# First expert tile's rows gathered from the route stage, with three weight matrices loaded behind that gather

## The reference, cut to what matters

```python
g_w, g_idx = lax.top_k(softmax(h @ w_gr + b_gr), 1)          # 1 of 4 groups
top_v, top_i = lax.top_k(softmax(e_logits of that group), 2) # 2 of its 8 experts
for e in range(32):
    hid = silu(h @ w_gate[e]) * (h @ w_up[e])                # 1024 -> 256
    out = out + combine[:, e:e+1] * (hid @ w_down[e])        # 256 -> 1024
```

## Time and profile before

| what | us |
|---|---|
| median of three runs | 1039.96 (1038.82 to 1040.89) |
| the profiled execution's own time | 1040.27 |
| its span, first to last recorded instruction | 1038.5 |
| route stage of layer 0, to the barrier | about 216.4 to 239.7 |
| expert stage of layer 0, until its pair rows are read back | about 239.7 to 488.9 |
| route stage of layer 1, to the barrier | about 740.7 to 763.6 |
| expert stage of layer 1, with the outputs | about 763.6 to 1038.5 |

### The profile page before, as it was taken

The page is one execution under the profiler, slowest core; times in us unless marked ns, Lnnn a source line. Parts: engine busy times, 40 slices in busy tenths (PEclk is TensorE's granted clock), DMA queues, the critical chain, the costliest instruction groups (busy, mean ns, idle before and its releaser), DMA issues. The chain is left out here.

```text
span 1038.5 us, 18756 instructions
## 1 busy us (share of the span) xinstructions
PE 906.1 (87%) x7250; PEld 658.1 (63%) x7250; DVE 414.2 (40%) x955; ACT 287.7 (28%) x595; POOL 293.3 (28%) x438
## 2 busy tenths in 40 slices
PE   7999999974999889875799999989849998887885
PEld 6988888963555555542687878579745555545553
DVE  5366784255111111111768878773552111111114
ACT  6356673131111111110532112362302111111103
POOL 1810000013343343211052527720123443443110
PEclk9999999996999999999589999999969999999997
DMA  7612111777999999996824636315869999999966
GB/s 234 187 36 52 51 42 54 272 300 295 373 416 416 417 413 415 418 420 237 266 67 127 159 85 159 92 50 220 359 256 362 414 415 418 416 415 419 420 277 254
DMA packets 112277, 277.71 MB, mean 267 GB/s; under 512 B 34952, under 2 KB 73176, under 8 KB 88074
## 3 DMA queue, kind: packets, MB, share of 16 engines
q1 hardware_dynamic: 96630, 253.74, 64.2%
q0 software_dynamic: 11424, 17.87, 4.7%
q10 hardware_dynamic: 4132, 4.86, 1.9%
HBM read 266.25 MB, written 27.45 MB: 283 GB/s over the span
## 5 line engine op out<-in xcount | busy, mean ns | idle before, releaser
L2106 DVE COPY areaB<-ps 128x512 f32<-128x512 f32 x66 | 45.6, 691 | 344.7 <-PE ps L2089 344.7
L2072 PE MATMUL ps<-ring,areaB 128*64 128x256 f32 x576 | 139.4, 397 | 24.6 <-issue 20.5
L2073 PE MATMUL ps<-ring,areaB 128*64 128x256 f32 x576 | 139.8, 398 | 0.0
L2118 POOL DMA_INDIRECT pair_rows<-areaB,idx x66 | 67.7, 1026 | 246.5 <-DVE areaB L2106 238.4
L2072 PEld LDWEIGHTS ps<-ring,areaB 128*64 128x64 f32 x576 | 79.0, 142 | 64.8 <-issue 25.2
L2097 ACT ACTIVATE v_rows<-ps 128x256 f32<-128x256 f32 x66 | 25.3, 384 | 256.5 <-PE ps L2073 256.5
L1058 PE MATMUL ps<-conv_x_high,pw_halves 128*128 128x272 f32 x512 | 90.1, 297 | 1.8 <-DVE areaS L1293 1.8
L2113 POOL DMA_INDIRECT areaC<-h_rows,idx x66 | 68.8, 1042 | 64.2 <-issue 45.8
L2094 ACT ACTIVATE areaB<-ps 128x512 f32<-128x512 f32 x66 | 39.4, 597 | 156.4 <-PE ps L2062 156.4
L2073 PEld LDWEIGHTS ps<-ring,areaB 128*64 128x64 f32 x576 | 79.0, 143 | 0.0
L2089 PE MATMUL ps<-ring,areaB 128*64 128x512 f32 x320 | 76.1, 593 | 2.7 <-DVE areaB L2103 1.6
(11 more groups left out here) (379 smaller groups left out, 1893.9 us busy)
## 6 DMA issues: line engine op xcount, KB each, us to landing
ring<-in_w_down SPq DMA_DIRECT2D x40, 1024.0 KB, 23.9
ring<-in_w_gate SPq DMA_DIRECT2D x32, 1024.0 KB, 23.7
ring<-in_w_up SPq DMA_DIRECT2D x32, 1024.0 KB, 26.4
wring<-in_w_down SPq DMA_DIRECT2D x12, 1024.0 KB, 25.7
areaS<-in_w_down SPq DMA_DIRECT2D x12, 1024.0 KB
wring<-in_w_pw SPq DMA_DIRECT2D x24, 512.0 KB, 4.6
areaA<-in_w_gate SPq DMA_DIRECT2D x10, 1024.0 KB, 27.1
areaA<-in_w_up SPq DMA_DIRECT2D x10, 1024.0 KB, 29.3
```

What stands on the lines that cost most here:

```text
L2072: pe.matmul(ps[0:CAP, 2 + odd, 0:F], rows, ring_gate(ws)[:, k, :], start=(k == 0), stop=(k == KT - 1))
L2073: mm = pe.matmul(ps[CAP:P, 2 + odd, 0:F], rows, ring_up(ws)[:, k, :], start=(k == 0), stop=(k == KT - 1))
L2106: return v.tensor_copy(rows_out[:, s, :], ps[:, 5 + odd, :])
L2118: return gp.indirect_dma_start(pair_half_rows, bass.IndirectOffsetOnAxis(idx[:, RING + s:RING + 1 + s], 0), rows_out[:, s, :], None, bound ...
```

## The change

GpSimd now issues tile 0's gather in the route stage, behind waits for the five stores and for `first_numbers`. That semaphore is raised by a new VectorE instruction which casts the first four columns of `tok_of` into `idx`, and stands between L1658 and L1659. In the expert stage GpSimd no longer casts for tiles 0 to 3, whose gathers follow each other without waits. SP no longer asks for down 4 and for gate and up 5 in the route stage; it does so first thing in the expert stage, after tile 0's gather has landed.

```diff
-        def half_row_numbers(v, steps, number, n, at):
+        def half_row_numbers(v, steps, number, n, at, first_numbers=None):
...
             steps.link(v.tensor_scalar(toks, toks, 2.0, half_col, ALU.mult, ALU.add))
+            if first_numbers:
+                v.tensor_copy(idx[:, 0:RIN], toks[:, 0:RIN]).then_inc(first_numbers, 1)
             steps.link(v.tensor_scalar(pairs, pairs, 2.0, half_col, ALU.mult, ALU.add))
...
+        def gather_rows(gp, s):
+            return gp.indirect_dma_start(rows_in[:, s, :], None, h_half_rows, bass.IndirectOffsetOnAxis(idx[:, s:s + 1], 0),
+                                         bounds_check=2 * T - 1, oob_is_err=False)
...
                     load_gateup(sp, l, 4, 4)
-                    load_down(sp, l, 4, 4)
-                    sp.wait_ge(h_stored, 16 * NT)
-                    load_gateup(sp, l, RING, RING)
...
                     gp.wait_ge(filled, 5)
+                    gp.wait_ge(h_stored, 16 * NT)
+                    gp.wait_ge(first_numbers, 1)
+                    gather_rows(gp, 0).then_inc(first_gathered[l], 16)
...
+                    sp.wait_ge(gathered[0], 16)
+                    load_down(sp, l, 4, 4)
+                    load_gateup(sp, l, RING, RING)
                     sp.wait_ge(fullest_ready, 1)
...
                     def fetch(x):
-                        after(gp, gathered[x.at], 16 * x.turns)
-                        fill_idx(gp, x.at, x.e, tok_ready, tok_of if x.e < RING else tok_seq, 0)
-                        after(gp, turned, x.e - RIN + 1)
-                        gp.wait_ge(tok_ready, x.e + 1)
-                        gather(gp, x.at).then_inc(gathered[x.at], 16)
+                        if x.turns:
+                            gp.wait_ge(gathered[x.at], 16 * x.turns)
+                            fill_idx(gp, x.at, x.e, tok_ready, tok_of if x.e < RING else tok_seq, 0)
+                            gp.wait_ge(turned, x.e - RIN + 1)
+                            gp.wait_ge(tok_ready, x.e + 1 - RIN)
+                            settle(gp, pool_settled)
+                        gather_rows(gp, x.at).then_inc(gathered[x.at], 16)
...
-                    for e in range(AHEAD):
+                    for e in range(1, AHEAD):
```

More of the change, by code:

```diff
@@ L1662, in hybrid_step, with make_table @@
         table = lambda bank: ps[:, bank, 256:256 + NE]
-        def make_table(v, steps, match_ready, table_made, n):
+        def make_table(v, steps, match_ready, table_made, n, first_numbers=None):
             match_slots(v, rank, match_ready)
             v.wait_ge(table_made, n + 1)
-            half_row_numbers(v, steps, table(3), NE, 0)
+            half_row_numbers(v, steps, table(3), NE, 0, first_numbers)
         def table_matmuls(pe, match_ready, j, table_made, bank):
@@ L1678, in table_matmuls @@
             mm.then_inc(table_made, 1)
+        first_gathered = {}
+        def gather_rows(gp, s):
+            return gp.indirect_dma_start(rows_in[:, s, :], None, h_half_rows, bass.IndirectOffsetOnAxis(idx[:, s:s + 1], 0),
+                                         bounds_check=2 * T - 1, oob_is_err=False)
         def route_stage(l, finished=()):
+            first_gathered[l], first_numbers = sem(f"rows_gathered{l}0"), sem(f"first_numbers{l}")
             std = areaB[:, 0:T - 256]
@@ L1856, in _ @@
                     s.link(v.tensor_copy(counts, count_cols))
-                    make_table(v, s, match_ready, table_made, 0)
+                    make_table(v, s, match_ready, table_made, 0, first_numbers)
         FULL, AGAIN = 18, 20
@@ L2031, in expert_stage @@
         def expert_stage(l):
-            gathered = [sem(f"rows_gathered{l}{s}") for s in range(RIN)]
+            gathered = [first_gathered[l]] + [sem(f"rows_gathered{l}{s}") for s in range(1, RIN)]
             scattered = [sem(f"rows_scattered{l}{s}") for s in range(RROW)]
@@ L2112, in gather @@
                 settle(gp, pool_settled)
-                return gp.indirect_dma_start(rows_in[:, s, :], None, h_half_rows, bass.IndirectOffsetOnAxis(idx[:, s:s + 1], 0),
-                                             bounds_check=2 * T - 1, oob_is_err=False)
+                return gather_rows(gp, s)
             def scatter(gp, s):
```

## The result

| kernel | median, us | runs | ratio to before, 95% interval |
|---|---|---|---|
| before | 1039.16 | 15 | |
| changed | 1043.32 | 15 | 1.0045 (1.0029 to 1.0061) |

The change makes the kernel slower, by 4.2 us at the medians. The profiled execution of the changed kernel has a span of 1041.2 us.

A forecast was written before the change was run, and what follows sets the result against it. The weight stream was taken to bound the kernel, through the hole before its unbroken part. Gains of 5.6 us in layer 0 and 3.9 in layer 1, taken as 9.6 together, gave 1030.4 us, range 1027.0 to 1035.6.

The forecast's parts named there:

- What bounds the kernel: Both expert stages: the weight stream at 416 GB/s ends each stage, so the hole ahead of its unbroken part matters.
- The barrier: End of the route stage: 0.53 us from VectorE's last step, so GpSimd goes on at 241.6 and 765.5.
- Gather 1's start: Start of the expert stage: 242.0 in layer 0 and 765.9 in layer 1, without cast or wait.
- signs of being wrong: Gather 1 landing above 4 us, GpSimd gaps above 1 us, second hole before gate and up 6, TensorE waiting for moved loads.
- Gather 1's landing: Expert stage, tile 1: 2.6 us, ahead of the weights by 1.6 us; bounds 2.5 and 8.7 us.
- rivals 2 and 3: Tile 1's gather: wholly behind weights, 6.8 us landing, 1039.5 us, chance 0.12; or 8.7 us landing, 1043.3 us, chance 0.06.
- 14.1 - 2x: Gain of both layers together in us, x being gather 1's time to land.
- Rival 3: Tile 1's turn, both layers: gather 1 lands in 8.7 us, kernel slower at 1043.3 us; chance 0.06.
- The rule beside the trace: DMA queues: engines alternate by whole packets, so a gather coming after the weights waits for them, whatever was asked first.
- the shift of the requests: Expert stages: requests waiting for TensorE come 5.6 us earlier in layer 0, 3.3 in layer 1; 8.9 us alone.
- the holes in the stream: Weight stream: old losses 10.4 and 12.5 us, less new holes 3.2 and 6.6 and later losses; 9.5 us, between 8.3 and 11.5.
- Rival 4: Route stage: gather 0 isn't ahead, GpSimd still waiting for stores or numbers; 1031.4 us, counted within the main case's 0.63.

The follow-up runs named there:

- the version without the drain: The changed kernel with GpSimd's drain instruction at the end of the route block left out in both layers; 1029.11 us, ratio to before 0.9901.
- down 4 in the hole: The changed kernel without GpSimd's drain at the route block's end, with down 4 asked for in the route stage again; 1030.62 us, ratio to before 0.9906.
- loads behind gather 1: The changed kernel, drain kept, with down 4 and gate and up 5 asked for after gather 1 instead of gather 0; 1034.84 us, ratio to before 0.9953.
- gathers 0 and 1 early: The changed kernel, drain kept, with gathers 0 and 1 both in the route stage and the three loads behind gather 1; 1032.44 us, ratio 0.9950.
- early gather alone: The changed kernel, drain kept, with the three loads back in the route stage, so gather 0 travels among weights; 1042.65 us, ratio to before 1.0039.
- all gathers behind barrier: The changed kernel, VectorE's cast and drain kept, with gather 0 back in the expert stage and the loads behind gather 1; 1030.46 us, ratio 0.9914.

## Why the prediction was wrong, point by point

- **What bounds the kernel**: right. The stream's rate is the same, and a shift of tile 0's product comes out at the end, within 2.3 us, in both directions.
- **The cast, gather 0's start**: right. 238.91 to 239.08 for the cast, 240.10 against 240.0 forecast.
- **The barrier: the step that failed.** The forecast took 0.53 us for it from VectorE's row and let GpSimd go on at 241.6. That row was of a barrier with nothing of GpSimd's under way, whose drain GpSimd had passed 20 us before. The changed kernel has gather 0 under way, and everyone went on at 243.6. What the gather has to wait for at its new place was asked of the stores and the numbers. What waits for the gather there, the block's end behind it, was given only the time of its issue. The branch of the block's end stood in the order of instructions quoted ahead of the prediction; what else happens there has no row in a trace in which it waits for nothing.
- **Gather 1's start**: 244.30 against 242.0, from the barrier alone. Layer 1, counted from the numbers, 4.9 us against 3.1. The gap of 2.92 us before it, the landing above 4 us and the second hole ahead of gate and up 6 were all named as signs of being wrong.
- **Gather 1's landing**: 7.6 us against 2.6. The mechanism was named, as rivals 2 and 3, and priced: 14.1 - 2x with x = 7.6 gives -1.1. With gather 1 starting 4.1 us late in the two layers together it is -5.2, and the sum of d moved by 5.05. What had no place among the rivals is what set them off. They had 0.18 between them, since the forecast took GpSimd for 1.6 us ahead and counted that if GpSimd is late, SP is too. The barrier broke that: it released both at the same time. Rival 3's time, 1043.3, is the one measured, but that is luck: it takes a gather 1 that starts on time and lands in 8.7 us, and gather 1 started 4.1 us late and landed in 7.6.
- **The lead that a gather needs** was too small in the forecast: it argued that the gather's descriptors need 1.0 us and the weights' bytes 1.4, so that even a gather level with SP's request would be ahead. The packet records show the first packet of a gather with nothing in its way 1.0 to 2.0 us behind its start, 1.7 in most, and that of the weights 0.95 to 1.2 us behind SP's request. A gather level with the request is behind, and a lead of about 1.1 us was needed (last section).
- **The rule beside the trace** that each DMA engine takes turns between queues by packets (the Trainium skill, "DMA: Bandwidth & Descriptors", section "Queues, rings and completion order") was weighed as speaking against the change, and the gather did wait: 7.6 us behind the weights, 2.8 with none. The trace agrees with turns from 248.8 us on, where packets of both queues alternate. Turns alone don't give what the forecast drew from them, that a later gather waits for all the weights ahead of it, and no run here shows why 1.48 MB went first.
- **The rest of the sum** was right, as the version without the drain shows: gather 1 at 241.44, tile 0's product 6.64 us behind the numbers (forecast 6.69) and 6.02 in layer 1 (6.71), the time 1029.1 (1030.4). Of the two ways to sum, the shift of the requests (8.9 us) and the holes in the stream (8.3 to 11.5), the first is the one that holds; down 4 in the hole brought nothing. One term was not as forecast: there the barrier opened 2 us sooner. That changed nothing, as gather 1 stands behind gather 0's issue in GpSimd's own list.
- **Rival 4**: the change did what it says. Gather 0 was ahead of the barrier and started 0.85 us sooner, and with the drain behind it that is what made it slow.

## What to carry to other kernels

An instruction that is moved ahead of a block's end is also moved into what that end waits for: if GpSimd has an indirect transfer under way there, all engines stand until it has landed. Move only the integers ahead and keep the transfer behind the barrier (8.3 us faster here), or put all transfers that the next stage's first work needs ahead of it (4.8). A small transfer that the critical path waits for should be a microsecond ahead of bulk loads, not merely in front of them; make the loads wait for the last of the small ones that the first work needs, not the first.

## What the runs showed of the hardware that I had not expected

- **The drain of GpSimd waits for the landing of its indirect transfers.** Idle time behind the last gather ahead of it: 2.92 us with no weights about, 6.83 with weights, 0.30 (the usual gap) when left out. The drain's own records, in us:

```
                             under way              layer 0   layer 1
changed                      gather 0                 3.50      3.05
loads behind gather 1        gather 0                 3.45      3.00
gathers 0 and 1 early        both                     4.23      3.78
early gather alone           gather 0, weights        7.41      6.86
all gathers behind barrier   nothing                  0.03      0.04
```

  Where a gather is under way, the drain ends 0.4 to 0.6 us behind the start of that gather's last packet.
- **Lead against landing.** The lead is SP's first request of a batch of three minus the gather's start, both from the timelines; negative means behind. These are gathers 1 to 3 of five of the kernels. Landings of 2.5 to 3.0 us, from a lead of 1.12 on, are the undisturbed trip.

```
lead, us     1.87  1.50  1.48  1.16  1.12  0.77  0.59  0.57  0.20  0.18  -0.01  -0.73
landing, us  2.8   3.0   3.0   2.5   2.5   4.9   5.7   6.4   7.1   7.1   8.1    7.6
```

- **Asking earlier among weights gains little.** With the loads in the route stage, gather 1 was asked for at 242.02 instead of 243.32, but tile 1's turn could start only at 249.57 instead of 250.16.
- **Why a lead of 1.1 us is enough and 0.8 is not** fits the packet records, though it wasn't tried apart. With a lead of 1.12 us the gather's packets start from 764.28 to 764.73, and the first of the weights is at 764.67. With 0.77 the gather's first is at 245.13, the weights' first at 245.39, and the gather's last at 247.89, among them. With 0.59 the weights' first is at 765.91 and the gather's first only at 768.00.
